# Hybrid GLA/Hyena encoder layer with 32 experts: gate-up weights of experts 5 to 31 loaded four chunks per transfer, features taken by fours

## What is computed

```python
for e in range(N_EXPERTS):                       # 32 experts
    gu = ht @ w_gate_up[e] + b_gate_up[e]        # w_gate_up[e]: 1024 x 2048 floats, 8 MB
    gate, up = gu[:, :D_FF], gu[:, D_FF:]
    gate = jnp.minimum(gate, SWIGLU_LIMIT)
    up = jnp.clip(up, -SWIGLU_LIMIT, SWIGLU_LIMIT)
    act = gate * jax.nn.sigmoid(SWIGLU_ALPHA * gate) * (up + 1.0)
    out = out + combine[:, e:e + 1] * (act @ w_down[e] + b_down[e])   # w_down[e]: 1024 x 1024, 4 MB
```

## Time and profile before

| What | Value |
|---|---|
| Median of three runs | 1307.4 us (1306.42 to 1308.09) |
| The profiled execution's own time | 1305.77 us |
| Its span, first to last instruction | 1304.0 us |
| Granted TensorE clock, mean | 0.990 |
| TensorE matmul busy | 1203.7 us (92%) |
| VectorE, ScalarE busy | 398.8 us (31%), 264.7 us (20%) |
| Read from HBM | 454.26 MB |
| Transfers of 2 MB | 122 of gate-up, 60 of down |

### The profile page before, as it was taken

The page is one execution under the profiler, slowest core; times in us unless marked ns, Lnnn a source line. Parts: engine busy times, 40 slices in busy tenths (PEclk is TensorE's granted clock), DMA queues, the critical chain, the costliest instruction groups (busy, mean ns, idle before and its releaser), DMA issues.

```text
span 1304.0 us, 14012 instructions
## 1 busy us (share of the span) xinstructions
PE 1203.7 (92%) x5992; PEld 619.1 (47%) x5992; DVE 398.8 (31%) x683; ACT 264.7 (20%) x398; POOL 0.2 (0%) x4
## 2 busy tenths in 40 slices
PE   7999999999999999999999988988898899889885
PEld 5889967888843343343334333322432243243322
DVE  6588837665631111121111111111111112111111
ACT  5765543344320010010001001000100010010001
POOL 0000000000000000000000000000000000000000
PEclk9999999999999989999999999999999989999998
DMA  9344423596589999999999999999999999999994
GB/s 326 111 152 120 139 65 97 201 376 194 194 334 382 429 426 428 428 427 428 428 428 427 426 430 426 428 428 428 427 428 428 428 427 427 430 426 427 430 425 187
DMA packets 64924, 456.25 MB, mean 350 GB/s; under 512 B 6650, under 2 KB 23323, under 8 KB 38749
## 3 DMA queue, kind: packets, MB, share of 16 engines
q1 hardware_dynamic: 63140, 454.51, 85.4%
q10 hardware_dynamic: 1720, 0.82, 0.2%
HBM read 454.26 MB, written 1.05 MB: 349 GB/s over the span
## 4 chain that ended last, share of the span: by engine, by line
PE 61%; DMA 29%; DVE 5%; ACT 3%; issue 2%; SPq 0%; ACTq 0%; DVEq 0%
DMA ring<-in_w_gate_up 28%; PE bank L1034 20%; PE bank L1050 12%; PE total L747 8%; PE bank L747 3%; PE total L735 3%; PE bank L790 3%; PE bank L735 2%; PE bank L1015 1%; PE bank L1041 1%; PE total L778 1%; PE bank L778 1%; PE bank L814 1%; ACT xn_area L1399 1%; PE total L1061 1%
## 5 line engine op out<-in xcount | busy, mean ns | idle before, releaser
L1034 PE MATMUL bank<-ring,hy_area 128*64 128x512 f32 x2048 | 457.2, 596 | 40.6 <-DMA ring<-in_w_gate_up 40.6
L1034 PEld LDWEIGHTS bank<-ring,hy_area 128*64 128x64 f32 x2048 | 139.9, 137 | 329.7 <-issue 247.8
L1050 PE MATMUL bank<-ring,xn_area 128*64 128x512 f32 x1024 | 233.6, 610 | 21.6 <-ACT xn_area L1399 21.6
L1797 DVE TENSOR_SCALAR qk_area<-bank 128x512 f32<-128x512 f32 x32 | 22.1, 692 | 424.8 <-PE bank L1034 424.8
L1050 PEld LDWEIGHTS bank<-ring,xn_area 128*64 128x64 f32 x1024 | 72.2, 140 | 161.6 <-issue 133.2
L1395 ACT ACTIVATE qk_area<-qk_area 128x512 f32<-128x512 f32 x32 | 20.2, 631 | 497.3 <-DVE qk_area L1797 497.3
L1813 DVE SCALAR_TENSOR_TENSOR xn_area_r<-bank,tmp_area,xn_area_r 128x512 fp32r<-128x512 f32 x32 | 24.0, 751 | 310.1 <-ACT xn_area_r L1404 310.1
L1503 DVE TENSOR_TENSOR front_r<-ring,slot_r 128x1024 fp32r<-128x1024 f32 x66 | 80.6, 1222 | 50.4 <-ACT slot_r L1238 50.4
L1238 ACT CAST slot_r<-ring 128x1024 fp32r<-128x1024 f32 x66 | 69.0, 1046 | 65.4 <-PE total L747 47.3
L1404 ACT ACTIVATE xn_area_r<-bank,tmp_area 128x512 fp32r<-128x512 f32 x32 | 22.0, 687 | 236.8 <-PE bank L1050 236.8
L814 PE MATMUL bank<-tmp_area_r 128*128 128x512 f32 x128 | 39.3, 429 | 8.5 <-DVE qk_area L1798 6.7
(11 more groups left out here) (323 smaller groups left out, 1206.1 us busy)
## 6 DMA issues: line engine op xcount, KB each, us to landing
ring<-in_w_gate_up SPq DMA_DIRECT2D x122, 2048.0 KB, 30.6
ring<-in_w_down SPq DMA_DIRECT2D x60, 2048.0 KB, 34.3
ring<-in_w_in SPq DMA_DIRECT2D x31, 1024.0 KB, 5.5
ring<-in_w_gate_up SPq DMA_DIRECT2D x12, 1024.0 KB, 8.9
ring<-in_w_down SPq DMA_DIRECT2D x8, 1024.0 KB, 21.3
ring<-in_w_branch_gla SPq DMA_DIRECT2D x4, 1024.0 KB, 6.5
ring<-in_w_branch_hy SPq DMA_DIRECT2D x4, 1024.0 KB, 5.7
ring<-in_w_out SPq DMA_DIRECT2D x4, 1024.0 KB, 4.9
```

Of the source, the lines that this page charges most:

```text
L1034: last = pe.matmul(banks[bk][half * CAP:(half + 1) * CAP, :], xeT[:, j, q, :], slot(where(j))[:, c:c + 512], start=False, stop=(j == GU_CH ...
L1050: last = pe.matmul(banks[2][half * CAP:(half + 1) * CAP, :], half_of(actT, f), slot(where(j))[:, c * D + half * 512:c * D + (half + 1) * 512],
```

## The change

Loads of n = 16 to 47 stay pairs. The gate-up chunks of experts 4 to 30 (the fifth to the last but one) come as transfers of four chunks, 4 MB, where partition p gets four neighbouring rows of `w_gate_up`, 32 KB in one piece. Their down chunks stay pairs, expert 31's gate-up chunks too, its down chunks stay single. The table `LOADS` lists (n, width), and `ARRIVAL` the semaphore and count of each chunk. A load of width w waits until `chunks_used` is at least n - 16 + w.

Since a slot must hold the same features for every expert, all gate-up loads, narrow ones too, now take their rows from a block of 512 rows of which partition p owns 4p to 4p + 3. A pair is half of such a 32 KB piece (16 KB), a single a quarter. `d_cols` therefore reads with a step of four floats, and the norm column is laid out by fours.

```diff
+def expert_loads():
+    loads, n = [], 0
+    while n < E * CH:
+        width = 1 if n < SLOTS or n >= E * CH - 4 else 2 if n < 4 * CH or n >= (E - 1) * CH or n % CH >= GU_CH else 4
+        loads.append((n, width))
+        n += width
+    return loads
...
+def expert_arrivals():
+    count, arrival = [0] * SLOTS, {}
+    for n, width in LOADS:
+        s = (n + MOE_SHIFT) % SLOTS
+        count[s] += 16
+        arrival.update({n + i: (s, count[s]) for i in range(width)})
+    return arrival
...
         def d_cols(d):
-            return slice(d // 2 * 2 * P + d % 2, (d // 2 + 1) * 2 * P, 2)
+            return slice(d // 4 * 4 * P + d % 4, (d // 4 + 1) * 4 * P, 4)
...
-            def pair_of(e, j):
+            def rows_of(e, j, width):
                 if j < GU_CH:
-                    return wgu[e, j * P:(j + 2) * P, :].rearrange("(p i) n -> p (i n)", i=2)
-                r = (j - GU_CH) * 2 * P
-                return wdn[e, r:r + 4 * P, :].rearrange("(p i) n -> p (i n)", i=4)
+                    r = j // 4 * 4 * P
+                    src = wgu[e, r:r + 4 * P, :].rearrange("(p i) n -> p (i n)", i=4)
+                    at = j % 4
+                else:
+                    r = (j - GU_CH) // 2 * 4 * P
+                    src = wdn[e, r:r + 4 * P, :].rearrange("(p i) n -> p (i n)", i=4)
+                    at = j % 2
+                return src[:, at * SLOT:(at + width) * SLOT]
...
-            for n in range(SLOTS, SINGLES_FROM, 2):
-                sp.wait_ge(chunks_used, n - SLOTS + 2)
-                moe_pair(n)
-            for n in range(SINGLES_FROM, E * CH):
-                sp.wait_ge(chunks_used, n - SLOTS + 1)
-                moe(n)
+            for n, width in LOADS[SLOTS:]:
+                sp.wait_ge(chunks_used, n - SLOTS + width)
+                moe(n, width)
...
-    parts += [a["norm2_w"].reshape(-1, P, 2).transpose(0, 2, 1).reshape(-1, P)]
+    parts += [a["norm2_w"].reshape(-1, P, 4).transpose(0, 2, 1).reshape(-1, P)]
```

More of the change, by code:

```diff
@@ L60 @@
 CH = GU_CH + DN_CH
-SINGLES_FROM = E * CH - 4
 MORE = SEQ // CAP - 1
@@ L134 @@
          ("wh1", "w_branch_hy", HALF)]
+def expert_loads():
[5 more added lines that the diff above has]
+    return loads
+LOADS = expert_loads()
+def expert_arrivals():
[5 more added lines that the diff above has]
+    return arrival
+ARRIVAL = expert_arrivals()
 TOKEN_MAJOR = ("v", "r", "gg", "wg", "gh", "wh", "wo")
@@ L578, in moe_arrival @@
         def moe_arrival(n):
[L580 to L584, removed]
+            s, count = ARRIVAL[n]
+            return moe_loaded[s], count
         def d_cols(d):
-            return slice(d // 2 * 2 * P + d % 2, (d // 2 + 1) * 2 * P, 2)
+            return slice(d // 4 * 4 * P + d % 4, (d // 4 + 1) * 4 * P, 4)
         wgu, wgub, wdn = ins["w_gate_up"], ins["b_gate_up"], ins["w_down"]
@@ L614, in front, with moe @@
                     sp.dma_start(front_tile(c), src).then_inc(front_arrival(c)[0], 16)
-            def pair_of(e, j):
+            def rows_of(e, j, width):
                 if j < GU_CH:
-                    return wgu[e, j * P:(j + 2) * P, :].rearrange("(p i) n -> p (i n)", i=2)
-                r = (j - GU_CH) * 2 * P
-                return wdn[e, r:r + 4 * P, :].rearrange("(p i) n -> p (i n)", i=4)
+                    r = j // 4 * 4 * P
[6 more added lines that the diff above has]
+                return src[:, at * SLOT:(at + width) * SLOT]
             def load_chunk(e, j, s, done):
-                sp.dma_start(slot(s), pair_of(e, j - j % 2)[:, j % 2 * SLOT:(j % 2 + 1) * SLOT]).then_inc(done, 16)
-            def moe(n):
+                sp.dma_start(slot(s), rows_of(e, j, 1)).then_inc(done, 16)
+            def moe(n, width=1):
                 s = (n + MOE_SHIFT) % SLOTS
[L629 to L634, removed]
+                sp.dma_start(ring[:, s * SLOT:(s + width) * SLOT], rows_of(n // CH, n % CH, width)).then_inc(moe_loaded[s], 16)
             for c in range(FSLOTS):
```

## The result

The changed kernel took **1312.3 us** (median of 16 runs, 1308.27 to 1314.1), the kernel before, run beside it, 1307.5 us (16 runs, 1304.67 to 1309.8). The ratio is 1.0030, 95% interval 1.0019 to 1.0041: slower by 0.3%, and above the forecast range of 1302.0 to 1309.2. The profiled execution took 1314.1 us (span 1312.3, granted clock 0.978), 8.3 us more than that of before (1305.8; 1304.0; 0.990). It is the longest of the 16 runs, so it shows more loss than the median's 4.8 us. Experts are counted from 0, as in the prediction, in all that follows; the title and the names of runs (from7, from9) count from 1.

The account below looks back on a forecast made before the run. DMA transfers were taken to set the pace from some 390 us on. Saved rows -2.5, later issue +0.5 and step 0 took the profiled 1305.8 to 1303.8 us, by median 1307.4 to 1305.4; range 1302.0 to 1309.2.

Parts of the forecast that it names:

- Step of four floats: The gather's 32 weight loads read `hn` at step four instead of two: taken as 0, ends 0 and 0.6 us.
- rival E: The step of four doubles a gather weight load, 3.8 us before the DMA stage starts: 1309.2 us, chance 0.06.
- Later issue: Expert 5's first four-chunk load (n = 60) waits for two more free slots: 0.5 us lost, bounds 0 and 2.1.
- the hole: Gap in the DMA stream near 488 us, before expert 5's first four-chunk load flows: 0.5 us, bounds 0 and 2.1.
- Fewer and longer rows: 54 four-chunk transfers replace 108 pairs, saving fixed row and closing-packet costs: 2.5 us saved, ends 0.5 and 5.9.
- rival B: Hardware cuts each 32 KB row into two 16 KB packets, saving only 0.5 us: 1307.4 us, chance 0.10.
- C: Rival: a row's fixed cost is higher than the line says, saving 5.9 us: 1302.0 us, chance 0.14.
- D: Rival: reads starting 32 KB apart run slower, 424 GB/s, 3.7 us lost on the four-chunk transfers: 1311.6 us, chance 0.10.
- Lumpy arrival: Four gate-up chunks become usable at once, every 9.8 us: costed at nothing, covered by TensorE's slack and the ring.
- The tail: Work after the last gate-up landing (last matmuls, activation, down chunks, final norm): 27 us, expected to keep its form.
- 2.5 us of slack per expert: While DMA sets the pace, TensorE needs 27.0 us per expert on average against DMA's 29.5: cover for lumpy arrival.

Follow-up runs that it names:

- e4: Changed kernel, but ScalarE and VectorE write `hn` so the gather's weight loads read contiguous floats (step of one): 1304.9 us, ratio 0.9997 to the kernel before.
- e3: Changed kernel with the gather's step put back to two floats, quads (four-chunk transfers) kept: 1304.8 us, ratio 0.9974 to the kernel before.
- e6: Changed kernel with `hn` stored in pieces of two neighbouring floats, so the gather reads at a step of two: 1306.8 us, ratio 0.9995 to the kernel before.
- e2: Changed kernel with every quad (four-chunk transfer) as two pairs, layout by fours and step of four kept: 1311.3 us, ratio 1.0036 to the kernel before.
- e9: Experts 0 to 7 as in the kernel before, experts 8 to 31 by fours with 46 quads (four-chunk transfers): 1304.6 us, ratio 0.9973 to the kernel before.
- e12: e9 with experts 28 to 31 back in the layout by twos, 40 quads (four-chunk transfers): 1303.0 us, ratio 0.9969 to the kernel before.
- e1: Kernel before with only the gather's weight reads changed to a step of four floats instead of two, no transfer changed: 1311.5 us, ratio 1.0037.
- e11: Kernel before with the gather's weights read at a step of eight floats: 1308.4 us in a single run.
- e5: Changed kernel with four-chunk transfers starting at expert 6 (the seventh) instead of expert 4, step of four kept: 1310.6 us, ratio 1.0030 to the kernel before.
- e8: Kernel before with the gather's weights read at a step of three floats: 1311.7 us in a single run.

## Why the prediction was wrong

**"Step of four floats", costed at 0 with ends 0 and 0.6, is the step that failed.** It is worth 3.4 us at the first gather (196 to 332 ns a load). The upper end came from the four transposes of the earlier trace rows, 0.66 against 0.73 us. They are another use: four instructions in which the time is mostly that of the matmul, and their step of four shows as 18 ns in the pace. Their own weight load records in the same trace were a warning: 140 ns in each group of transposes at one float (L712), 211 at four (L1041). The nearest row of the same operation was the earlier trace rows, weight loads at a step of two with 0.12 us between them. I read these as "as slow as the slow form", and compared them with no weight load at a step of one. The trace of the kernel before has such loads in the projections of its front part, whose stationary operand is 128 neighbouring floats:

```profile
L747 PEld LDWEIGHTS bank<-slot_r,xn_area_r x44: 186/188/190, 29.0 to 353.2; 128*128 128x128 f32 x44
```

188 ns there, and 187 in e4, against 196 at a step of two: two is the fast form, and that could be read beforehand. The rival E had mechanism and price right (3.8 us forecast, 3.4 measured) and got a chance of 0.06. A factor of two was the honest upper end of the range for this term, since the trace had no row of this use at this step, and the rule of 16-byte lines spoke for it.

**"Later issue", 0.5 us with 2.1 as its end, was mis-sized twice.** Alone, in e3, the hole took 20 x (424 - 392) / 428 = 1.5 us over 480 to 500, and 2.0 by the whole stage (1277.1 - 399.55 = 877.6 against e6's 875.55). I let the queued data end at the landing of n = 58, 489.5 less a little. With 2.1 us for the start of a transfer, that put the last moment for the issue without a hole at 487.0, 89.7 us behind n = 24; by the table it is 88. A landing waits for the last of 16 engines, and the mean engine is dry earlier: in the changed kernel n = 58 was issued at 473.8 and landed 22.7 us later, at 496.5, while the rate fell to 66 GB/s at 494, and in e3 it landed at 491.1, with the rate down from 488.5 on. And the term was worked out with the fast gather: the second slow gather adds 3.45 us to the same interval, which makes 3.5 us of hole by the windows. A cost in one term was the input of another.

**"Fewer and longer rows", 2.5 us, was right in kind and too small.** Rows go whole (rival B is out), and 9 ns are saved per row instead of 4.7: 54 x (8 x 9 + 9) ns = 4.4 us; e6 shows 4.2 and e4 4.0. The line through the 2 KB rows gave too little, the truth lies between it and C.

**Right**: from 390 us on DMA sets the time, and a delay ahead of it goes through undiminished (e2: +3.3 at n = 24, +3.2 at the last landing). Reads from farther apart cost nothing (D, shown by e2). Lumpy arrival cost nothing: in e6, e9 and e12 the rate stays at 430 GB/s. The tail kept its form: 25.2 us in e6, 26.9 before, 28.2 now, with 7.11, 8.79 and 10.02 us for the last down chunks by the clock there. What "2.5 us of slack per expert" left out: a slow gather takes 3.45 us of the lead that TensorE regains, and faster transfers take more of it; in e9 and e3 the slack is gone at the end.

**The sum with the measured sizes** is 3.4 - 4.2 + 3.9 = +3.1 us, where 3.9 is the hole by the whole stage (879.5 less 875.55), of which some 0.9 us (91.6 less 90.7) is half clock between the two issues. The median says +4.8 (2.5 to 5.4 by the interval, which holds the 3.1). That the rest, if it is one, goes with the clock is a guess that no run shows.

## What to carry to other kernels

Before the layout in SBUF is changed for the sake of a DMA, look at who reads that tile, with which operand, and at which step: price a strided weight load by rows of weight loads at that step, and where there are none take a factor of two as the upper end. A cost ahead of a DMA-bound stage is paid in full, and the same cost behind it is free as long as the lead holds (e12), so a change that is good for the transfers and bad for the engine should begin and end where the lead covers it. For the moment at which a queue is dry, count bytes at the mean rate, not the landing of its last transfer.

## What was not expected of the hardware

**Half clock in short stretches, more of them after the change.** Over all runs the mean granted clock was 0.987 for the kernel before (77 runs, those beside e1 to e11) and 0.979 for the changed one (16), 0.980 for the step alone and 0.975 for e6. A single stretch moved the profile of the changed kernel by 2.8 us because it fell on expert 0's down chunks, 32 matmuls (9.86 for 7.09 us) that stand bare ahead of the DMA stage. The traces of e5 and e8 have it there too (9.65 and 10.04 us), the other eleven do not. The 16 runs of the changed kernel lie in two groups, six at 1308.3 to 1309.5 and ten at 1310.8 to 1314.1. That this stretch is what parts them is likely and not shown, since only one run has a profile, and the mean clock does not order them (1309.45 us had 0.973, 1312.88 us 0.980); why the changed kernels are granted less was not found either.

**ScalarE and VectorE pay for a step of four too**: 2.13 for 1.15 us per 1024 columns on ScalarE (e4, which reads `x` at a step of four and writes without gaps), and 2.17 for 1.28 on VectorE, there in two instructions, so moving the stride from TensorE to them does not remove it.
